# A split output projection: three passes in place of one full-precision product, with the weights' halves made by ScalarE and the Pool engine

## The reference, cut to what matters

```python
def moba_mixer(h, w_qkv, w_o, q_gain, k_gain, pos):
    B, S, D = h.shape
    q, k, v = jnp.split(h @ w_qkv, 3, axis=-1)
...
    q = rotary(rms_norm(q, q_gain), pos)
    k = rotary(rms_norm(k, k_gain), pos)
    o = moba_attention(q.transpose(0, 2, 1, 3), k.transpose(0, 2, 1, 3), v.transpose(0, 2, 1, 3))
    return o.transpose(0, 2, 1, 3).reshape(B, S, D) @ w_o
```

## Time and profile before

| | |
|---|---|
| median of 3 runs | 1630.87 us (1629.05 to 1631.75) |
| the profiled execution | 1630.74 us, span 1628.9 us, mean granted clock of TensorE 0.895 |
| TensorE busy | 1265.6 us (78%) |
| VectorE busy | 632.5 us (39%) |
| ScalarE busy | 417.1 us (26%) |
| Pool busy | 15.6 us (1%) |
| output projection `w_o` on TensorE | from 672.69 to 700.41 us |

### The profile page before, as it was taken

One profiled execution on the slowest core, in us unless ns is written; L12 is line 12 of the kernel. 1 busy time (PEld: TensorE's weight loads), 2 busy tenths in 40 slices (PEclk: granted clock), 3 DMA queues, 4 the chain that ended last, 5 costly groups with the idle time before them and its releaser, 6 DMA issues.

```text
span 1628.9 us, 18030 instructions
## 1 busy us (share of the span) xinstructions
PE 1265.6 (78%) x7602; PEld 909.9 (56%) x7602; DVE 632.5 (39%) x1084; ACT 417.1 (26%) x607; POOL 15.6 (1%) x31
## 2 busy tenths in 40 slices
PE   1999898899998797889999888484845646646645
PEld 1998785399886386579888467353412212312212
DVE  3487523367542358547642046934201001101102
ACT  4353330243332343434332221332100000000001
POOL 2000000000000000000000000000000000000000
PEclk9999998899999899999999998697878777878878
DMA  6343358335455344135454433054399999999976
GB/s 220 117 155 120 139 189 328 108 124 190 156 206 181 123 153 153 40 120 195 168 183 155 166 104 131 1 218 195 146 430 427 428 430 427 430 427 429 428 328 232
DMA packets 97755, 362.44 MB, mean 222 GB/s; under 512 B 7145, under 2 KB 10436, under 8 KB 85780
## 3 DMA queue, kind: packets, MB, share of 16 engines
q1 hardware_dynamic: 95792, 356.10, 56.6%
q0 software_dynamic: 1536, 3.58, 0.8%
q10 hardware_dynamic: 356, 1.73, 0.3%
HBM read 360.35 MB, written 1.05 MB: 222 GB/s over the span
## 4 chain that ended last, share of the span: by engine, by line
PE 54%; DMA 20%; DVE 12%; ACT 3%; issue 2%; SPq 1%; DVEq 0%; ACTq 0%
PE bank L840 25%; DMA arena<-in_exp_w 20%; PE bank L822 10%; PE bank L605 7%; PE bank L812 2%; PE bank L788 2%; PE bank L1104 1%; PE bank L1065 1%; PE bank L1096 1%; DVE low_w L1466 1%; SPq L2363 1%; ACT arena L2060 1%; ACT hT L2087 1%; PE bank L1252 1%; SPq L2422 1%
## 5 line engine op out<-in xcount | busy, mean ns | idle before, releaser
L605 PE MATMUL bank<-arena 128*32 128x512 f32 x944 | 197.6, 707 | 97.1 <-DMA arena<-in_exp_w 94.8
L1466 DVE TENSOR_TENSOR low_w<-ring,split_high 128x2048 fp32r<-128x2048 f32 x76 | 171.4, 2289 | 114.2 <-ACT split_high L2075 114.2
L840 PE MATMUL bank<-turned_high,low_w 128*128 128x256 f32 x720 | 206.7, 287 | 0.0
L2075 ACT ACTIVATE split_high<-ring 128x2048 fp32r<-128x2048 f32 x76 | 142.3, 1909 | 116.6 <-DMA ring<-in_w_down 62.2
L822 PE MATMUL bank<-ring,hT 128*128 128x512 f32 (+1 forms) x352 | 156.0, 605 | 14.6 <-ACT hT L2085 8.4
L2060 ACT ACTIVATE arena<-bank 128x512 f32<-128x512 f32 (+1 forms) x143 | 81.1, 595 | 333.2 <-PE bank L840 130.3
L605 PE MATMUL bank<-ring,arena 128*32 128x512 f32 x528 | 92.1, 682 | 80.9 <-DMA arena<-in_exp_w 80.9
L840 PE MATMUL bank<-turned_high,split_high 128*128 128x256 f32 x512 | 147.6, 288 | 8.0 <-DVE turned_low L1475 8.0
L840 PE MATMUL bank<-turned_low,split_high 128*128 128x256 f32 x512 | 147.2, 288 | 0.0
L605 PEld LDWEIGHTS bank<-arena 128*32 128x32 f32 x944 | 53.6, 127 | 166.1 <-issue 166.0
L840 PEld LDWEIGHTS bank<-turned_high,low_w 128*128 128x128 f32 x720 | 141.4, 196 | 0.0
(11 more groups left out here) (392 smaller groups left out, 1887.9 us busy)
## 6 DMA issues: line engine op xcount, KB each, us to landing
arena<-in_exp_w SPq DMA_DIRECT2D x59, 2048.0 KB, 22.9
ring<-in_exp_w SPq DMA_DIRECT2D x33, 2048.0 KB, 20.2
ring<-in_w_up SPq DMA_DIRECT2D x16, 2048.0 KB, 8.7
ring<-in_w_down SPq DMA_DIRECT2D x16, 2048.0 KB, 7.9
ring<-in_mod_w SPq DMA_DIRECT2D x12, 2048.0 KB, 8.4
ring<-in_w_in_ar SPq DMA_DIRECT2D x7, 2048.0 KB, 8.5
ring<-in_w_qkv SPq DMA_DIRECT2D x6, 2048.0 KB, 8.1
ring<-in_ple_gate SPq DMA_DIRECT2D x4, 2048.0 KB, 7.9
```

Of the source, the lines that this page charges most:

```text
L605: last = mm(mb[bank][strip(e), :], act[:, k, strip(e)], w[e][:, k, cols], start=(k == 0), stop=(k == n_k - 1), skip_group_check=True)
L840: last = mm(dst, *pair, start=(start and i == 0), stop=(stop and i == 2))
L1466: v.tensor_tensor(low_of(name, s), half_of(slot(name), name, s), high_of(name, s).bitcast(F32), ALU.subtract).then_inc(sem("split_low"), 1)
L2075: nc.scalar.activation(high_of(name, s), half_of(slot(name), name, s), ACT.Copy)\
```

## The change

The output projection goes through `split_tokens`. Its inputs' high half is what ScalarE copies from the banks "o" (to `turned_high`); VectorE makes their low half by a subtraction (`context_low`), two of the four inside the rounds of the attention. ScalarE makes the high halves of the two `w_o` units between the last `qkv` evacuation and the copies of queries and keys. The Pool engine makes their low halves, and issues its two transfers for layer 1 behind them. The transposed probabilities move from page 16 to page 12, since page 16 is now a buffer of high halves. The split units are numbered with two more among them, so the second feed-forward's first high halves wait for the `w_o` units.

```diff
-        prob, probT = blocks(page(14, 2), 8), page(16).rearrange("p (b k q) -> p b k q", b=4, k=2)
+        prob, probT = blocks(page(14, 2), 8), page(12).rearrange("p (b k q) -> p b k q", b=4, k=2)
...
             if l == 0:
-                split_units += [("qkv", c) for c in range(6)]
+                split_units += [("qkv", c) for c in range(6)] + [("w_o", c) for c in range(2)]
...
             def half_ready(name, s):
 
-                pe.wait_ge(sem("split_low"), 2 * split_no[name] + s + 1)
+                if name[0] == "w_o":
+                    pe.wait_ge(sem("out_low"), 2 * name[1] + s + 1)
+                else:
+                    pe.wait_ge(sem("split_low"), 2 * (split_no[name] - (2 if name[0] in ("up", "down") and name[1] else 0))
+                               + s + 1)
                 return high_of(name, s), low_of(name, s)
...
             for c in range(4):
                 banks.wait_read(pe, "att", "o", c)
-            token_units(("w_o",), 2, hT3)
+            for c in range(2):
+                split_tokens(("w_o", c), ("w_o", c))
             feed_forward(1)
...
                         v.tensor_scalar(part, part, rinv[:, i2:i2 + 1], None, ALU.mult).then_inc(sem(tag + "_prob"), 1)
+                    if tag == "att" and i in (10, 14):
+                        context_low((i - 10) // 4)
+                if tag == "att":
+                    context_low(2)
+                    context_low(3)
+
+            def context_low(c):
+                cols = slice(c * 512, (c + 1) * 512)
+                bank = banks.read(dve, "att", "o", c)
+                dve.wait_ge(sem("context_high"), c + 1)
+                v.tensor_tensor(turned_low[:, cols], bank.ap, turned_high[:, cols].bitcast(F32), ALU.subtract)\
+                    .then_inc(bank.freed, 1)
...
                         if i2 >= 5 and (i2 - 5) % 4 == 0:
-                            c = (i2 - 5) // 4
-                            evacuate(dst[:, 2 * c:2 * c + 2, :], ACT.Copy, tag, "o", c)
-                evacuate(dst[:, 6:8, :], ACT.Copy, tag, "o", 3)
+                            keep_context((i2 - 5) // 4, tag, dst)
+                keep_context(3, tag, dst)
+
+            def keep_context(c, tag, dst):
+                if dst is None:
+                    bank = banks.read(act, tag, "o", c)
+                    s.activation(turned_high[:, c * 512:(c + 1) * 512], bank.ap, ACT.Copy).then_inc(sem("context_high"), 1)
+                else:
+                    evacuate(dst[:, 2 * c:2 * c + 2, :], ACT.Copy, tag, "o", c)
...
                     evacuate(dst[:, t, (u % 2) * 512:(u % 2 + 1) * 512], ACT.Copy, "qkv", u, t, scale=rstd[:, t:t + 1])
+            for c in range(2):
+                split_high("w_o", c)
             for tag, dst in (("qT", qT), ("kT", kT)):
                 for c in range(4):
                     evacuate(dst[:, 2 * c:2 * c + 2, :], ACT.Copy, tag, c)
-            attend("att", prob, probT, hT3)
+            attend("att", prob, probT, None)
...
             for l in range(2):
                 if l:
-                    pool.wait_ge(sem("ple_added"), 1)
+                    for c in range(2):
+                        name = ("w_o", c)
+                        for s_half in range(2):
+                            pool.wait_ge(sem("split_high"), 2 * split_no[name] + s_half + 1)
+                            nc.gpsimd.tensor_tensor(low_of(name, s_half), half_of(slot(name), name, s_half),
+                                                    high_of(name, s_half).bitcast(F32), ALU.subtract)\
+                                .then_inc(sem("out_low"), 1)
                 pool.dma_start(p_tok, a["p"][l, 0].rearrange("(t p) n -> p t n", p=P)).then_inc(sem("p_landed"), 16)
```

## The result

The changed kernel takes 1636.79 us (median of 7 runs, 1634.90 to 1638.09), the kernel before 1630.87 in as many. The ratio is 1.0037, with a 95% interval from 1.0025 to 1.0048: slower, by 5.9 us. A second set of seven runs at the end of the study gave 1.0042 (1.0027 to 1.0056). The profiled execution took 1637.47 us, its span 1635.7.

The account below looks back on a forecast made before the run. No one engine bounds the kernel: in the attention they take turns, TensorE holding 54% of the last-ending chain. Terms -5.9 + 5.9 + 0.4 + 1.05 + 0.6 + 4.2 = +6.2 us on 1630.9 gave 1637.1, range 1632.0 to 1642.0.

Parts of the forecast that it names:

- The four copies in front: ScalarE's four upper-half copies, ahead of the query and key copies, delay the first query copy and all behind: 5.9 us lost.
- The Pool engine: Its four weight subtractions, 4.3 us each, block VectorE's scalings in the attention: 4.2 us lost.
- The half clock at the attention's start: TensorE idles about 7 us while ScalarE copies, so the attention starts at a lower clock: 0.4 us lost.
- The context's lower halves: Four new VectorE subtractions of 128x512: 1.05 us lost inside the attention's rounds, 0.6 us at the end before the projection.
- The projection: The output projection's 64 records in 27.72 us become 96 matmuls of 0.227 us, 21.8 us: a gain of 5.9.
- The rival "the projection starts at half the clock": TensorE begins the output projection at half clock after idling, 1.7 us more, 1638.8; chance 0.12.
- Carrying each microsecond to the end: A first-block delay moves the final experts' weight transfers equally, so every microsecond lost or gained reaches the total time.
- The covers for SyncE's loads, the Pool engine's transfers and the next layer's upper halves: Later loads and the next layer's first upper halves stay hidden behind other work, costing nothing; uncovered, the halves cost 4.5 us.

Follow-up runs that it names:

- e7: Kernel before plus only ScalarE's four 128x2048 copies at the change's place, results unread, and the transposed probabilities in page 12; 1.0023 of the kernel before.
- e1: Changed kernel with the weights' four lower-half subtractions on VectorE, between key rotation and attention, instead of the Pool engine; 1.0005 of the kernel before.
- e8: Kernel before plus only four 128x2048 Pool engine subtractions beside the attention, results unread; 1.0091 of the kernel before.
- e2: Changed kernel with each of the Pool engine's four subtractions cut into four of 128x512; 1.0039 of the kernel before.
- e3: Changed kernel with ScalarE's copies moved to where it is idle and all lower halves on VectorE, none on the Pool engine; 0.9993 of the kernel before.
- e5: As e3, but the projection's first half waits only for the context's first two pieces; 0.9969 of the kernel before.
- e6: As e3, with two useless 128x512 matmuls where TensorE waits for the context's last pieces; 0.9976 of the kernel before.
- e4: As e3, but with the weights' lower halves on the Pool engine, the first unit's meeting the key rotation; 1.0060 of the kernel before.

## Why the prediction was right, and where it was not

The prediction was 1637.1, the time is 1636.8. The two main steps are shown by runs, but the agreement to 0.3 us is luck: to the projection's end alone the profile has +8.5 us where the sum has +6.2, the later stages add 1.9, and the timed executions show less than either.

- *The four copies in front*: 5.9 predicted, 5.7 in the chain. Right, and e7 shows them alone at 6.1 with the clock behind them.
- *The Pool engine*: operations of 4.3 us predicted, 4.49 measured; stops of 4.2, measured 3.9, one short and one of 3.3 net, where they were placed. Right. e1 takes them away, e8 makes four of them, e2 shrinks them. The 4497 ns of the Trainium skill ("GPSIMD Engine Reference", section 3.1), which the prediction quotes beside it, was closer for the operation, and the runs agree with it. The stops that it gives, 1.1 and 3.3 us, were not: 0.65 and 3.28.
- *The half clock at the attention's start*: 0.4 predicted; 0.2 us ahead of the first score operation and 0.26 in the first round. In e7, which has neither Pool work nor lower halves, 6.1 less the copies' 5.7 leaves as much.
- *The context's lower halves*: 1.05 in the rounds and 0.6 behind them predicted; e3 shows 1.6 and 0.85. Under-sized: the slack of 0.2 us that I took off twice wasn't there to take, since a wait for TensorE of 0.18 us still stands behind the first of them, and at the tail the round ends that much later.
- *The projection*: a gain of 5.9 predicted, 4.1 measured. The step that failed is the largest mis-sized term of the sum: it took the pace of a stage at full clock for a stage that ran 3.4 us at 1.2 GHz, which cost 1.6 us. The other 0.25 is that 96 matmuls take 22.05 us at full clock from first start to last end, not 96 times 0.227. The rival "the projection starts at half the clock", at 0.12, is what happened, in all three profiles, at the 1.7 us named for it. e5 and e6 show that it doesn't happen without the idle time ahead of the projection; e1 and e2, with 1.74 and 1.75 us of it at full clock, show that the idle time is not all that decides.
- *Carrying each microsecond to the end*: wrong. The later stages took 1.9 us more in the profiles of the changed kernel, and 2.6 less in e7.
- The covers for SyncE's loads, the Pool engine's transfers and the next layer's upper halves held: none of them is in the chain.

With the terms as measured the stretch is 5.7 + 0.2 + 5.8 + 0.8 - 4.1 + 1.9 = 10.3 us longer, and three profiles say 10.4. The timed difference is 5.9 to 6.8, its upper bounds 7.8 and 9.1. The profiled executions, 1637.5, 1641.3 and 1636.2 against 1630.7 and 1629.9, don't settle it. The granted clock on record for each execution gives a hint: in the changed kernel its mean is 0.885, 0.886 and 0.887 in the three profiled executions and 0.888 to 0.892 in all twelve that were only timed, while the kernel before has 0.893 and 0.895 profiled and 0.890 to 0.897 timed. So TensorE had a higher clock in the timed executions of the changed kernel than in those that the stretch was read from. In which stage, and whether that makes up the whole difference, isn't shown. The number was right because the gain that was overrated, the loss at later stages and a loss that doesn't arrive in full in the timed executions cancel.

## What to carry to other kernels

Before moving elementwise work to the Pool engine, look at what VectorE does meanwhile. Where it was on the path with scalings from SBUF to SBUF, or with operations on two tiles in SBUF, each Pool instruction of 4.5 us that met one cost 3.0 to 4.3 us here, except where it was nearly over (0.65). Work put "beside" a stage belongs ahead of that stage's last evacuation in the engine's program, not behind it. When a stage of TensorE is made shorter, see that the wait ahead of it doesn't grow (1.0 us became 1.84 here), and let its first part start on the inputs that are ready: with three passes that was worth 3.4 us, with the direct product nothing.

## What the runs showed of the hardware

- 32 products of 128x128 by 128x512 in full precision took 27.7 us, in three passes 22.05 us at 2.4 GHz (from first start to last end) and 23.65 when 3.4 us of it ran at 1.2 GHz.
- A subtraction of 128x2048 took 4.49 us on the Pool engine and 2.29 on VectorE.
- A Pool subtraction of 128x2048 stopped VectorE's scalings from SBUF to SBUF (0.29 and 0.35 us became up to 3.89) and its tensor_tensor on two SBUF tiles (0.69 became 4.98); operations that read a bank kept their length. In the profile the stop shows as a longer instruction, not as idle time.
- 1.84 us without work ahead of a dense stage, behind an attention with gaps, came with the half clock on it in the changed kernel and in e3, 1.75 us in e4; 1.74 and 1.75 us in e1 and e2 didn't, nor did 1.0 us in the direct kernel. Two matmuls in the gap, or no gap, kept the clock at 1.00 throughout.
- From the first query projection to the second block's output projection, the clock's pattern repeated from one profile of a kernel to the next (two of one kernel, three of the other), and edits at one stage changed what the stages up to 370 us later took: 375.2, 377.9, 379.8 or 381.0 us for the same instructions. Timed executions of one kernel needn't share one pattern: in e1 three of twelve were some 7 us longer, at a mean clock lower by 0.004 to 0.010.
